# Recurrent heads of a two-block layer stack: lags on column groups, pairwise blocks over four levels, output and norm placed among the projections

## The reference

```python
log_f = jnp.log(lb + (1.0 - lb) * jax.nn.sigmoid(z))      # forget gate f, per key dimension
k = (1.0 - lb) * jax.nn.sigmoid(-z)
qf = jax.nn.silu(q.astype(f32))
...
    b = jnp.cumsum(lfc, axis=2)
    rel = b[:, :, :, None, :] - b[:, :, None, :, :]
    decay = jnp.exp(jnp.where(causal[:, :, None], rel, -jnp.inf))
    scores = jnp.einsum('bhtk,bhtsk,bhsk->bhts', qc, decay, kc)
    o_intra = jnp.einsum('bhts,bhsv->bhtv', scores, vc)
...
o = o * lax.rsqrt(jnp.mean(o * o, axis=-1, keepdims=True) + NORM_EPS)
o = o.reshape(B, S, HG_WIDTH) * norm_g.astype(f32) * jax.nn.silu(g.astype(f32))
```

## Time and profile before

| | |
|---|---|
| median of 3 timed runs | 1895.97 us (1895.9 to 1906.71) |
| profiled execution, its own time | 1896.23 us |
| its span | 1894.1 us, 34175 instructions |
| granted TensorE clock, mean | 0.932 |
| busy share: PE, PEld | 89%, 77% |
| busy share: DVE, ACT, POOL | 44%, 30%, 13% |
| bytes read | 430.63 MB, 229 GB/s over the span |

### The profile page before, as it was taken

How to read it: one execution, slowest core, us unless ns; L and a number is a source line. 1 busy time by engine, 2 the same in 40 slices (tenths; PEclk the granted TensorE clock), 3 DMA queues, 4 the chain that set the end, 5 groups by cost and what they waited for, 6 DMA issues and landing times.

```text
span 1894.1 us, 34175 instructions
## 1 busy us (share of the span) xinstructions
PE 1686.0 (89%) x14334; PEld 1460.7 (77%) x14335; DVE 835.5 (44%) x1525; ACT 572.1 (30%) x865; POOL 243.2 (13%) x208
## 2 busy tenths in 40 slices
PE   8999979676677777758999999999999999999996
PEld 6888948543333433428999989999999999899996
DVE  1215152411111111136656765755675567566554
ACT  2000040211001000015434555533453345554432
POOL 1000020000000000012111162111111112611111
PEclk9898969699888888878999999999999999999998
DMA  8422204389999999991455655355545556444551
GB/s 359 178 101 100 101 0 146 132 359 426 426 427 426 426 427 426 426 395 67 172 195 180 254 198 182 133 190 186 209 154 187 188 210 236 167 167 167 182 186 56
DMA packets 40299, 433.22 MB, mean 229 GB/s; under 512 B 4475, under 2 KB 4603, under 8 KB 5252
## 3 DMA queue, kind: packets, MB, share of 16 engines
q1 hardware_dynamic: 39460, 427.49, 57.8%
q0 software_dynamic: 736, 4.22, 0.6%
HBM read 430.63 MB, written 3.16 MB: 229 GB/s over the span
## 4 chain that ended last, share of the span: by engine, by line
PE 57%; DMA 18%; DVE 6%; ACT 2%; issue 1%; POOL 1%; DVEq 0%; POOLq 0%; SPq 0%; ACTq 0%
DMA ring<-moe_w_dram 18%; PE bank L768 15%; PE bank L770 15%; PE bank L769 15%; PE bank L478 3%; PE bank L733 2%; PE bank L750 1%; PE bank L910 1%; DVE h_lo L1444 1%; POOL area L441 1%; PE bank L929 1%; DVE lo_last L1452 0%; DVE lo_first L1452 0%; DVE stat L1432 0%; PE bank L915 0%
## 5 line engine op out<-in xcount | busy, mean ns | idle before, releaser
L768 PE MATMUL bank<-h_hi,w_hi 128*128 128x256 f32 x1792 | 511.8, 286 | 9.6 <-DVE h_lo L1444 7.8
L769 PE MATMUL bank<-h_lo,w_hi 128*128 128x256 f32 x1792 | 504.7, 282 | 0.0
L768 PEld LDWEIGHTS bank<-h_hi,w_hi 128*128 128x128 f32 x1792 | 339.1, 189 | 14.3 <-issue 9.3
L769 PEld LDWEIGHTS bank<-h_lo,w_hi 128*128 128x128 f32 x1792 | 339.2, 189 | 0.3
L770 PE MATMUL bank<-h_hi,lo_last 128*128 128x256 f32 x1088 | 306.8, 282 | 0.0
L1176 ACT CAST w_hi<-ring 128x2048 fp32r<-128x2048 f32 x120 | 228.4, 1903 | 76.2 <-PE bank L770 60.3
L770 PEld LDWEIGHTS bank<-h_hi,lo_last 128*128 128x128 f32 x1088 | 206.3, 190 | 0.0
L769 PE MATMUL bank<-hid_lo,w_hi 128*128 128x256 f32 x704 | 197.8, 281 | 0.0
L768 PE MATMUL bank<-hid_hi,w_hi 128*128 128x256 f32 x704 | 197.8, 281 | 0.0
L770 PE MATMUL bank<-h_hi,lo_first 128*128 128x256 f32 x704 | 197.8, 281 | 0.0
L733 PE MATMUL bank<-ring,area 128*32 128x256 f32 x2048 | 123.9, 381 | 73.6 <-DMA ring<-moe_w_dram 49.6
(11 more groups left out here) (321 smaller groups left out, 2414.1 us busy)
## 6 DMA issues: line engine op xcount, KB each, us to landing
ring<-moe_w_dram SPq DMA_DIRECT2D x128, 1536.0 KB, 25.5
ring<-layer_w_dram SPq DMA_DIRECT2D x120, 1536.0 KB, 6.5
ring<-first_w_dram SPq DMA_DIRECT2D x22, 1536.0 KB, 6.9
bias_copies_dram<-bias_rows_dram POOLq DMA_DIRECT2D x1, 2048.0 KB, 11.0
x_t<-x_dram SPq DMA_DIRECT2D x1, 1024.0 KB, 4.8
area<-bias_copies_dram POOLq DMA_DIRECT2D x1, 1024.0 KB, 9.3
out_dram<-h_t SPq DMA_DIRECT2D x1, 1024.0 KB, 3.9
consts<-consts_dram SPq DMA_DIRECT2D x1, 603.5 KB, 8.0
```

What stands on the lines that cost most here:

```text
L768: pe.matmul(out_ap, a_hi, b_hi, start=start, stop=False, **flags)
L769: pe.matmul(out_ap, a_hi, b_lo, start=False, stop=False, **flags)
```

## The change

Four things, all between the first value unit and the attention.

1. **Lags.** `diagonal(d)` now has `band_p` moving (256 tokens) and, as weights, a window of 32 columns of the constant `one_row` in which only column d is ones. The four heads go to the four groups of 32 columns of the array, and the 16 lags add up in one half of `ps[4]`: row 32h+d is lag d of head h. Afterwards ScalarE copies it (`copy_band`), TensorE transposes it (`turn_band`), and VectorE masks, reduces and spreads it straight into `hg_scores`.
2. **Blocks by halves.** In place of 15 steps over growing key ranges, four levels with n = 16, 32, 64, 128: in each pair of neighbouring runs of n tokens, late queries meet early keys. VectorE scales the late half of `q_hg` and the early half of `k_hg` by the total decay of the other run before the next level. ScalarE copies the diagonal pieces out (`copy_levels`, eight copies).
3. **Places.** TensorE calls `quarter(u, n)` after each quarter of a unit from unit 6 on; tables say what is done there: lags at quarters 1 to 21, transposes at 25, levels at 27, 33, 35 and 37, output at 42, sums at 46 (counted from unit 6; the last unit ends at 64).
4. **Output and norm** come before the attention on every engine, and the tables `extra` are gone. The output's second product takes only the 128 late columns of the late tokens. `proj_done` is told by the last product of a unit, ahead of a step at its last quarter. `AREA` shrinks by 512 to make room for `one_row`.

```diff
+def quarter_at(n):
+    return 6 + n // 4, n % 4
+
+BAND_AT = [quarter_at(2 * d + 1) for d in range(6)] + [quarter_at(d + 6) for d in range(6, SUB)]
+TURN_AT = quarter_at(25)
+LEVEL_AT = [quarter_at(n) for n in (27, 33, 35, 37)]
+HG_OUT_AT, HG_SUMS_AT = quarter_at(42), quarter_at(46)
...
                 pe.wait_ge(S("band_p_ready"), d + 1)
                 for h in range(HG_HEADS):
-                    for j in range(TT):
-                        c = (h * TT + j) * SUB + d
-                        last = pe.matmul(ps[4][:, c:c + 1], band_p[:, d % 2, h, j * P:(j + 1) * P], ones[:, 0:1],
+                    last = pe.matmul(ps[4][WIN * h:WIN * (h + 1), 0:T], const("one_row")[:, WIN - 1 - d:2 * WIN - 1 - d],
+                                     band_p[:, d % 2, h, :], start=d == 0, stop=d == SUB - 1)
+                last.then_inc(S("band_done"), 1)
...
+            def level(m):
+
+                pe.wait_ge(S("level_ready"), m + 1)
+                if m == 3:
+                    pe.wait_ge(S("band_copied"), 1)
+                n = SUB << m
+                for h in range(HG_HEADS):
+                    if m == 3:
+                        last = pe.matmul(ps[5][:, h * P:(h + 1) * P], k_hg[:, h, 0:P], q_hg[:, h, P:T],
                                          start=True, stop=True)
-                last.then_inc(S("band_done"), 1)
-
-            def earlier(i):
-
-                if i == 1:
-                    pe.wait_ge(S("band_copied"), 1)
-                    pe.wait_ge(S("bias_row_ready"), 1)
-                pe.wait_ge(S("kdec_ready"), i)
+                    for j in range(TT if m < 3 else 0):
+                        late_t = q_hg[:, h, j * P:(j + 1) * P].rearrange("p (c two l) -> p c two l", two=2, l=n)[:, :, 1, :]
+                        at = (2 * h + j) * (P // 2)
+                        last = pe.matmul(ps[(6, 7, 4)[m]][:, at:at + P // 2].rearrange("p (c l) -> p c l", l=n),
+                                         k_hg[:, h, j * P:(j + 1) * P], late_t, start=True, stop=True)
+                last.then_inc(S("level_done"), 1)
...
-            pe.wait_ge(S("hg_scores_ready"), 1)
-            for h in range(HG_HEADS):
-                for j in range(TT):
-                    last = pe.matmul(half(6 + h // 2, h % 2), vtok[:, j, h * P:(h + 1) * P], hg_scores[:, h, j, :],
-                                     start=j == 0, stop=j == TT - 1)
-            last.then_inc(S("hg_o_ready"), 1)
...
+            ahead = {BAND_AT[-1][0]: copy_band, LEVEL_AT[-1][0]: copy_levels, HG_OUT_AT[0]: copy_hg,
+                     HG_SUMS_AT[0]: lambda: root("hg_var_ready", 1, sq[:, 4:8, :], sq[:, 4:8, :], "hg_std_ready")}
             for u, (what, b0) in enumerate(projection_units()):
+                if u in ahead:
+                    ahead[u]()
                 act.wait_ge(S("proj_done"), u + 1)
...
+            for m in range(1, 4):
+                n = SUB << (m - 1)
+                total = decays[:, (m - 1) % 2, 0:4 * T // n].rearrange("p (b two) -> p b two", two=2)
+                dve.wait_ge(S("level_done"), m)
+                late_q = q_hg[:, :, :].rearrange("p h t -> p (h t)").rearrange("p (b two l) -> p b two l", two=2, l=n)
+                early_k = k_hg[:, :, :].rearrange("p h t -> p (h t)").rearrange("p (b two l) -> p b two l", two=2, l=n)
+                if m < 3:
+                    own.mark(tt(decays[:, m % 2, 0:2 * T // n], total[:, :, 0], total[:, :, 1], ALU.mult))
+                own.mark(tt(late_q[:, :, 1, :], late_q[:, :, 1, :], over(total[:, :, 0], n, 2), ALU.mult))
+                own(tt(early_k[:, :, 0, :], early_k[:, :, 0, :], over(total[:, :, 1], n, 2), ALU.mult))
+                dve.sem_inc(S("level_ready"), 1)
...
+            hg_variance()
+            for h in range(HG_HEADS):
+                hg_norm(h)
             dve.wait_ge(S("bias_loaded"), 16)
-            attention({2: hg_variance, 4: lambda: hg_norm(0), 5: lambda: hg_norm(1),
-                       6: lambda: hg_norm(2), 7: lambda: hg_norm(3)})
+            attention()
```

More of the change, by code:

```diff
@@ L492, in folded_sums, with attention @@
                     last.then_inc(S("sum_ready"), 1)
-            def attention(extra):
+            def attention():
                 def score(h):
@@ L571, in _, with turn_band @@
-            between = [lambda d=d: diagonal(d) for d in range(SUB)] + [lambda i=i: earlier(i) for i in range(1, NSUB)]
+                    last = pe.matmul(ps[4][WIN * h:WIN * (h + 1), 0:T], const("one_row")[:, WIN - 1 - d:2 * WIN - 1 - d],
+                                     band_p[:, d % 2, h, :], start=d == 0, stop=d == SUB - 1)
+                last.then_inc(S("band_done"), 1)
+            def turn_band():
+                pe.wait_ge(S("band_rows_ready"), 1)
+                pe.wait_ge(S("bias_row_ready"), 1)
+                for j in range(TT):
+                    last = pe.transpose(ps[5][:, j * P:(j + 1) * P], band_rows[:, j * P:(j + 1) * P], ident)
+                last.then_inc(S("band_turned"), 1)
@@ new lines, in hg_out @@
+            def hg_out():
+                pe.wait_ge(S("hg_scores_ready"), 1)
+                pe.wait_ge(S("proj_read"), 8)
+                for h in range(HG_HEADS):
+                    bank = 6 + h // 2
+                    pe.matmul(half(bank, h % 2), vtok[:, 0, h * P:(h + 1) * P], hg_scores[:, h, 0:2, :],
+                              start=True, stop=False, skip_group_check=True)
+                    last = pe.matmul(ps[bank][:, h % 2 * T + P:(h % 2 + 1) * T], vtok[:, 1, h * P:(h + 1) * P],
+                                     hg_scores[:, h, 2, :], start=False, stop=True, skip_group_check=True)
+                last.then_inc(S("hg_o_ready"), 1)
@@ new lines, in hg_sums @@
+            def hg_sums():
+                pe.wait_ge(S("hg_sq_ready"), 1)
+                for h in range(HG_HEADS):
+                    last = pe.matmul(half(6 + h // 2, h % 2), ones, sq[:, h, :], start=True, stop=True)
+                last.then_inc(S("hg_sum_ready"), 1)
+            steps = {BAND_AT[d]: lambda d=d: diagonal(d) for d in range(SUB)}
+            steps[TURN_AT] = turn_band
+            steps.update({LEVEL_AT[m]: lambda m=m: level(m) for m in range(4)})
+            steps[HG_OUT_AT], steps[HG_SUMS_AT] = hg_out, hg_sums
@@ L572, in _, with quarter @@
+            def quarter(u, n):
+                if (u, n) in steps:
+                    steps[u, n]()
             for u, (what, b) in enumerate(projection_units()):
@@ L586, in _ @@
                                                start=k == 0, stop=k == KB - 1)
+                            if side == TT - 1 and k == KB - 1:
+                                last.then_inc(S("proj_done"), 1)
+                            if k % 4 == 3:
+                                quarter(u, 2 * side + k // 4)
                 else:
@@ L594, in _ @@
                                 m.then_inc(S("slot_used"), 1)
+                            if k == 3:
+                                quarter(u, 2 * j)
                         last = pe.matmul(half(u % 4, j), ones[0:1, :], b_v[:, b * VCOLS:(b + 1) * VCOLS],
                                          start=False, stop=True)
-                last.then_inc(S("proj_done"), 1)
-                if u >= 6:
-                    for _ in range(2):
-                        if between:
-                            between.pop(0)()
-            for step in between:
-                step()
-            pe.wait_ge(S("hg_scores_ready"), 1)
-            for h in range(HG_HEADS):
-                for j in range(TT):
-                    last = pe.matmul(half(6 + h // 2, h % 2), vtok[:, j, h * P:(h + 1) * P], hg_scores[:, h, j, :],
-                                     start=j == 0, stop=j == TT - 1)
-            last.then_inc(S("hg_o_ready"), 1)
-            def hg_sums():
-                pe.wait_ge(S("hg_sq_ready"), 1)
-                for h in range(HG_HEADS):
-                    last = pe.matmul(half(6 + h // 2, h % 2), ones, sq[:, h, :], start=True, stop=True)
-                last.then_inc(S("hg_sum_ready"), 1)
+                        if j == TT - 1:
+                            last.then_inc(S("proj_done"), 1)
+                        quarter(u, 2 * j + 1)
             pe.wait_ge(S("proj_read"), FIRST_UNITS)
-            attention({1: hg_sums})
+            attention()
             pe.wait_ge(S("o_copied"), MB_HEADS)
@@ L1577, in _ @@
-            m.then_inc(S("hg_scores_ready"), 1)
+            own(dve.tensor_copy(g[:, :, 0], q[:, :, 0]))
+            own.mark(tt(q, g, over(f[:, :, 0], SUB, 2), ALU.mult))
+            w = subs(sq[:, 0:4, :])
+            own(dve.tensor_copy(w[:, :, SUB - 2], f[:, :, SUB - 1]))
+            for t in range(SUB - 3, -1, -1):
+                own(tt(w[:, :, t], w[:, :, t + 1], f[:, :, t + 1], ALU.mult))
+            own.mark(tt(k[:, :, 0:SUB - 1], k[:, :, 0:SUB - 1], w[:, :, 0:SUB - 1], ALU.mult))
```

107 lines of the change are left out of this document (42 added, 65 removed).

## The result

The changed kernel took 1837.62 us (median of 4 runs, 1837.38 to 1838.2), the kernel before 1901.34 beside it (4 runs, 1895.9 to 1907.44). The ratio is 0.9679, 95% interval 0.9656 to 0.9702: faster by 3.2%. The prediction was 1841. The profiled execution took 1838.2 (span 1836.2) against 1896.23 (span 1894.1), from which the prediction counted: 58.0 less, where 55.7 were forecast. The ratios leave out runs over 1.5% above the fastest of their kernel, which concerns two of the ten of old_lags only.

The account below looks back on a forecast made before the run. TensorE was taken to bound the kernel until the first attention score: that stretch 141.8 us for 194.2, gain 52.4, plus 3.3 in the attention, 55.7 off 1896.23, gives 1840.5, say 1841; range 1830 to 1855.

Parts of the forecast that it names:

- The bound: TensorE bounds the stretch until 248.06 us; a microsecond saved before 282.33 counts as one saved at the end.
- The lags: Sixteen lags among the projections at 0.75 us each, 0.3 of it for changing array shape both ways; 12.0 us.
- Rival (b): Lags: column groups behind full-array work go one after the other, 33 us instead of 12.0, total 1862; chance 8%.
- The levels: The four levels among the projections: 56 instructions of 0.112 us, 6.3 us together.
- No step waits: Steps among the projections: the chains on VectorE and ScalarE all have cover, so none makes TensorE wait.
- rival (d): A late chain stops TensorE or pushes the norm into the attention; costs 12 us, total 1853; chance 12%.
- The clock: TensorE's clock stays full through the projections, so 14.2 us of projection work done at half clock goes.
- rival (c): Projections: the clock still dips, at short steps instead of long ones; the 14.2 us stay, total 1855; chance 8%.
- (e): Slower: steps at the units' quarters hold the clock at 1.2 GHz from unit 6 on; total 1976 us; chance 3%.
- Output, sums, wait: Before the attention: output products 2.7 us, sums of squares 1.8, waiting for ScalarE to read the last unit 1.0.
- The attention: From first score to first output product: 31 us, mostly at half clock, against 34.3 before; gain 3.3.
- Rival (a): The attention starts after unbroken products and keeps the full clock: 8 us less, total 1833; chance 12%.

Follow-up runs that it names:

- old_lags: The changed kernel with the lags put back to 8 products of one column each, VectorE copying the band; 1878.3 us, ratio 0.9886.
- one_group: The changed kernel with the four heads' lag products all on the first 32 columns of the array, four small ScalarE copies; 1858.2 us, ratio 0.9776.
- wide_lags: old_lags with 64 equal columns moving in each lag product instead of one; 1858.4 us, ratio 0.9779.
- new_lags_only: The kernel before with only the lags' new form, ScalarE's copy and two transposes; 1869.3 us, ratio 0.9828.
- filled_start: The changed kernel with six useless full products on TensorE at the attention's start only; 1835.8 us, ratio 0.9651.
- norm_in_attention: The changed kernel with sums, variance, root and norm back in the attention's steps, output left among the projections; 1838.4 us, ratio 0.9677.
- late_output: The changed kernel with the output product after the last projection unit, sums and norm in the attention; 1840.5 us, ratio 0.9679.
- filled_attention: The changed kernel with 15 useless full products on TensorE spread over the attention; 1830.0 us, ratio 0.9630.

## Why the prediction was right, step by step

**The bound.** TensorE's order was the path until the first score, and shifting it shifted the end: 57.7 us at the first output product, 57.9 in the span. That everything after would shift by one amount was wrong in detail (60.1, then 57.4). The absolute time was met within 3.4 us of the median; the kernel before has its own runs 12 us apart.

**The lags.** Forecast 0.75 each and 12.0; measured 0.57 at the eight places after a bias product, where the engine changes shape anyway, and 0.74 to 0.77 at the eight others. From 53.91 to 109.05 the lags make 10.9 us beyond the projections' own 44.2. The full price of changing shape had been added at all sixteen. The Trainium skill's rule that a change of tiling mode drains the engine ("TensorEngine Tiling (Array Packing)", Key Properties) agrees with 0.17 us on the work around a lag and 0.13 on the lag itself. Rival (b) was tested and is out: serial groups are what one_group shows, 21 us.

**The levels.** 0.108 an instruction (1.73 over 16), forecast 0.112; three of 1.73 and one of 0.89 are 6.1 for 6.3.

**No step waits.** True for all 23 steps; rival (d) did not occur.

**The clock.** The 14.2 us of dips went entirely; rival (c) is out, and so is (e), for the clock stayed at 1.00 with a lag at ten quarters in a row. The prediction took them as a side matter of 14 us, a sum read from one execution. The runs show more behind it: the one-column products lower the clock by an amount that changes from one execution to the next: old_lags lay between 4 and 34 us above the median of wide_lags. For the 16-column products it is only argued, from the dips behind them in new_lags_only. That the kernel before scatters over 12 us for the same reason, and the changed one over 1 because it lacks both, is only argued too, and filled_start, which lacks both as well, scatters over 7.5.

**Output, sums, wait.** 2.6 and 1.7 for the forecast 2.7 and 1.8, and the wait for ScalarE 0.93 for 1.0. The stretch: 139.7 for 141.8, so 54.5 gained where 52.4 were forecast.

**The attention.** 31.0 for the forecast 31, in part by luck. Half clock and its pace were right: the first transposes came 4.84 after the first score (4.7), two steps took 2.41 and 2.82 (2.4 each), three 3.88 (3.89), with no wait between. But 1.4 had been taken off for a start at the full level, and the start ran 0.6 longer than worked out at half clock. The last part, carried over from the kernel before as 11.2, took 9.3, and this hid it. Two things shorten it. The clock is back from 222 on, and the norms no longer stand in it: in filled_start, also without norms but at half clock to the end, it is 10.2 (215.17 to 225.39), with the norms in norm_in_attention 11.2. With the wait of 0.89 the norms thus cost some 2 us of the attention.

Of the gain of 3.3, 1.5 is there by the first transposes, 6.3 us after the first score in the kernel before and in late_output and 4.8 in norm_in_attention: ScalarE no longer has the output's squares and copies to make ahead of the first exponential. The price of the sums, 1.8, had been set against it in the other term, so the total was right. Rival (a) came true in no run of the change; filled_attention shows it was worth 5.4 us in the attention where 8 were named.

## What to carry to other kernels

A product of one column cost here as much as one of 64, 0.11 us an instruction with 128 columns of weights, and in this program a second time through the clock: put the long operand on the moving side, the short one in the weights, and let small outputs share the array by column groups. Work placed early under other work is worth only the wait that it removes; here that was under 1 us of 58. The rest was less work on the engine that bounds, its waits for a long chain on VectorE, and its clock. Where a chain of short steps leaves TensorE at half its clock, useless products in its waits can pay: 7.6 us for 15 of them, 12.6 with 70 more, by the medians. Six at the start alone did not change the attention's time. And a forecast that meets the time can still be made of parts that miss: check each term against its own row.

## What was not expected of the hardware

Ten runs of one program (old_lags) on one chip lie 30 us apart, in step with the mean granted clock (0.937 to 0.920), and 64 moving columns in place of one shrink that to 5 us. How a mean clock of 0.920 was spread over the projections stays open: only the fastest execution has a trace. TensorE can leave the full array for four products on column groups and return in the middle of an accumulation for 0.3 us in all (0.17 and 0.13). And the same instructions from the second layer norm's first sums to the end took from 1047.8 us (the change) to 1049.9 (late_output), so that differences of 2 us in this kernel's total say nothing of an edit before it.
